# The w_down product of a decoder layer's MLP: 19 of its 44 steps over pairs of k tiles by Strassen's seven block products

## The chip, the cores and the metric

One Trainium2 chip, of which the kernel uses one core. The metric is the device time of one execution in microseconds (us), as the median of several runs. Engines are named as in the profile: PE (TensorE, the matmuls), PEld (its weight loads), DVE (VectorE), ACT (ScalarE), POOL (GpSimd), SP (SyncE, which here issues the loads).

## What is computed

One hybrid decoder layer on a sequence of 256 tokens and 2048 channels, in float32: two attention branches, then a gated MLP with a causal convolution. The change concerns only the last line of it, the product with w_down:

```python
D_MODEL = 2048; SEQ = 256; D_FF = 5632
...
        h = rms_norm(x, ffn_norm_g)
        u = causal_depthwise_conv(h @ w_up, conv_w, conv_b)
        gate, val = jnp.split(u, 2, axis=-1)
        x = x + (jax.nn.silu(gate) * val) @ w_down
    return x
```

## The kernel before

Every weight matrix streams through the same four-slot pipeline of chunks. A chunk is 128 partitions by 1024 float32 columns (512 KB). SP loads it into `raw[slot]`; ACT copies it to `hi[slot]` in the rounded matmul format (line 417); DVE subtracts, `lo = raw - hi` (line 740); PE then uses both. A float32 product is made of three matmuls with 512 moving columns: x_hi with w_hi, x_lo with w_hi, x_hi with w_lo, added up in one PSUM bank. All of PE's matmuls of the stage are recorded at line 1346 (`mm`). The semaphores that order this are counts over all chunks: `w_landed` (load finished), `hi_done`, `lo_done`, and `w_used` (PE has finished with the chunk). SP loads chunk c once `lo_done` shows that the chunk before it in the same slot has been split; ACT's split of chunk c waits until PE has used chunk c - 4. So the splits run at most three chunks ahead of PE.

The left operand of the w_down product is `ffT`: 44 tiles (k) of 128 channels by 256 tokens, its hi parts in columns 0 to 255 and its lo parts in columns 256 to 511. The product has two halves m of 1024 output columns. In each, PE goes over the 44 k tiles, one chunk of w_down each, and for each makes 4 products (2 token halves t by 2 column groups g), of 3 matmuls each, into the four banks `A[2 * t + g]`: 12 matmuls a chunk. At the end of a half DVE adds each bank to `y`, which holds the residual (`add_rows`, line 1103), and the first matmul of a bank in half 1 waits for that addition (`free_down`). SP stores `y` last. The banks `B` stand idle in this stage.

During the first eleven chunks of the stage the end of the up-projection still runs beside it (`up_step`): POOL multiplies the last four tiles (lines 1310, 1313, 1327, 1331), DVE does the convolution's taps (line 1051) and splits the last tiles of `ffT` (line 1058), ACT writes their hi parts (line 687).

```python
            for m in range(2):
                ...
                for k in range(FT):
                    if m == 0:
                        pe.wait_ge(ffT_done, k + 1)
                    rows_chunk(C_DOWN + FT * m + k + 1, k % SLOTS, ffT, [k], BLOCK,
                               [(A[2 * t + g], t, g * GRP, (g + 1) * GRP)
                                for t in range(TH) for g in range(2)], k == 0,
                               k == FT - 1, free_down, down_full)
```

Of the kernel before, what the change touches and what calls it, by code (L numbers as in the profile page):

```python
# [20 lines left out]

# [7 lines left out]
def hybrid_layer(nc, x, positions, attn_norm_g, w_in, q_norm_g, k_norm_g, w_branch, w_out,  # L29
# [9 lines left out]
    P = 128  # L39
# [35 lines left out]
    C_DOWN = C_UP + NU * 2 * CPG  # L75
    for first in (C_ROWS, C_HEADS, C_GATES, C_BRANCH, C_OUT, C_UP, C_DOWN):
        assert first % SLOTS == 0
# [9 lines left out]
    with ctx:  # L87
# [111 lines left out]
        silu = [at(f"silu{i}", [S], U0 + (13 + i) * KB) for i in range(4)]  # L199

# [130 lines left out]
        out_ready = sem("out_ready")  # L331
# [25 lines left out]
        def _(sp):  # L357
# [37 lines left out]
            with sp.Fori(0, 2) as m:  # L395
                load_group(C_DOWN, w_down, FT * m, BLOCK * m, n=FT, width=BLOCK, per=1)
            for m in range(2):
                for t in range(TH):
                    for h in range(2):
                        cols = slice(m * BLOCK + h * GRP, m * BLOCK + (h + 1) * GRP)  # L400

                        sp.wait_ge(out_ready, 4 * m + 2 * t + h + 1)
                        sp.dma_start(out[0, t * P:(t + 1) * P, cols], y[:, t, cols])\
                            .then_inc(stored, 16)
# [4 lines left out]
        def _(act):  # L409
# [312 lines left out]
            LAST = 3 * SLOTS  # L722
            for j in range(LAST):
                split(C_DOWN + AHEAD + j)
                up_step(NU, j)
            left = 2 * FT - AHEAD - LAST
            with act.Fori(0, left // SLOTS) as r:
                for j in range(SLOTS):
                    split(C_DOWN + AHEAD + LAST + j, r)
            for j in range(left - left % SLOTS, left):  # L730
                split(C_DOWN + AHEAD + LAST + j)


        @block.vector
        def _(dve):
# [357 lines left out]
            LAST = 3 * SLOTS  # L1093
            for j in range(LAST):
                split(C_DOWN + AHEAD + j)
                up_step(NU, j)

            def add_rows(m):
                for t in range(TH):
                    for g in range(2):  # L1100
                        cols = y[:, t, m * BLOCK + g * GRP:m * BLOCK + (g + 1) * GRP]
                        wait_full(dve, down_full, m, 4, 2 * t + g, C_DOWN + FT * (m + 1))
                        dve.tensor_tensor(cols, A[2 * t + g][:, :], cols, ALU.add)\  # L1103
                            .then_inc(out_ready, 1)

            first = C_DOWN + AHEAD + LAST
            with dve.Fori(0, (FT - LAST) // SLOTS) as r:
                for j in range(SLOTS):
                    split(first + j, r)
            add_rows(0)  # L1110
            second = first + FT - LAST
            left = FT - AHEAD
            with dve.Fori(0, left // SLOTS) as r:
                for j in range(SLOTS):
                    split(second + j, r)
            for j in range(left - left % SLOTS, left):
                split(second + j)
            add_rows(1)


        @block.gpsimd
        def _(pool):
# [217 lines left out]
            val_tiles(NU - 1)  # L1340


        @block.tensor
        def _(pe):
# [313 lines left out]
            for m in range(2):  # L1658
                def free_down(o):
                    if m == 0:  # L1660
                        pe.wait_ge(col_done, 64 + 4 * NU)
                    else:
                        pe.wait_ge(out_ready, 4 * (m - 1) + o + 1)
                for k in range(FT):
                    if m == 0:
                        pe.wait_ge(ffT_done, k + 1)
                    rows_chunk(C_DOWN + FT * m + k + 1, k % SLOTS, ffT, [k], BLOCK,
                               [(A[2 * t + g], t, g * GRP, (g + 1) * GRP)
                                for t in range(TH) for g in range(2)], k == 0,
                               k == FT - 1, free_down, down_full)  # L1670
# [22 lines left out]
```

## Time and profile before

| | |
|---|---|
| median of 3 runs | 1466.05 us (1465.93 to 1466.65) |
| the profiled execution's own time | 1466.32 us |
| its span, first to last instruction | 1464.3 us |
| PE busy | 1455.5 us, 99% of the span, 7688 matmuls |
| DVE busy | 932.5 us, 64% |
| ACT busy | 768.0 us, 52% |
| POOL busy | 431.1 us, 29% |
| mean DMA traffic | 186 GB/s |
| granted PE clock, mean | 0.999 |

Matmuls overlap in the pipeline, so one has a recorded duration of about 390 ns while they start much closer together; the pace has to be read from the starts. A busy share is an average over stages; what counts for this change is what the engines do in the last 240 us, where the w_down product runs. In the rows, "idle before" is the time an engine stood still before an instruction, with what released it.

### The profile page before, as it was taken

The numbers are of one execution on the slowest core, as the hardware profiler recorded it, in microseconds if no ns is written. First come the engines' busy times: TensorE is split into PE (matmuls) and PEld (weight loads), VectorE is DVE, ScalarE is ACT, GpSimd is POOL, SyncE is SP. The second block draws the span as 40 slices with busy tenths as digits, with TensorE's granted clock in tenths as the row PEclk, the third lists the DMA queues.
The fourth block names the chain that finished last, engine by engine and source line by source line (L and its number), as shares of the span: only waits on it lengthen the run. The fifth ranks groups of instructions, "written<-read, shape, count | busy, mean of one in ns | idle before, by whom it ended". The sixth has DMA issues, their size and how long they took to land.

```text
span 1464.3 us, 24546 instructions
## 1 busy us (share of the span) xinstructions
PE 1455.5 (99%) x7688; PEld 1246.4 (85%) x7688; DVE 932.5 (64%) x1205; ACT 768.0 (52%) x1063; POOL 431.1 (29%) x486
## 2 busy tenths in 40 slices
PE   8999999999999999999999999999999999999999
PEld 6888888888888888888888888888888888888887
DVE  6545455876655557765567778777777777545443
ACT  6544445576766766655454554454554555333332
POOL 1100000323222223550015555655555655000000
PEclk9999999999999999999999999999999999999999
DMA  7666665655555555575566666666666666655554
GB/s 243 194 181 186 186 180 165 193 179 177 158 167 158 158 169 176 186 246 186 186 186 177 198 188 186 185 187 194 193 188 192 179 191 198 201 194 191 190 197 147
DMA packets 130489, 272.09 MB, mean 186 GB/s; under 512 B 10784, under 2 KB 10816, under 8 KB 130192
## 3 DMA queue, kind: packets, MB, share of 16 engines
q1 hardware_dynamic: 129664, 269.12, 59.8%
q0 software_dynamic: 464, 2.42, 0.5%
q8 instruction: 25, 0.41, 0.1%
q14 instruction: 16, 0.13, 0.0%
q10 hardware_dynamic: 320, 0.01, 0.0%
HBM read 269.42 MB, written 2.10 MB: 185 GB/s over the span
## 4 chain that ended last, share of the span: by engine, by line
PE 99%; DVE 0%; DMA 0%; ACT 0%; issue 0%; POOL 0%; DVEq 0%; ACTq 0%; POOLq 0%
PE bank L1346 98%; PE bank L1395 0%; DMA rows_in<-in_attn_norm_g 0%; PE bank L1529 0%; DVE y L1103 0%; PE bank L1569 0%; DVE hT L765 0%; PE bank L1489 0%; ACT hi L417 0%; ACT hT L434 0%; POOL rows_in L1123 0%; DVE lo L740 0%; PE bank L1446 0%; PE bank L1419 0%; PE bank L1476 0%
## 5 line engine op out<-in xcount | busy, mean ns | idle before, releaser
L740 DVE TENSOR_TENSOR lo<-raw,hi 128x1024 fp32r<-128x1024 f32 (+1 forms) x508 | 651.0, 1285 | 425.0 <-ACT hi L417 424.2
L417 ACT ACTIVATE hi<-raw 128x1024 fp32r<-128x1024 f32 (+1 forms) x508 | 535.3, 1055 | 540.9 <-PE bank L1346 536.5
L1346 PE MATMUL bank<-h2T,hi 128*128 128x512 f32 x1408 | 482.8, 394 | 0.0
L1346 PE MATMUL bank<-h2T,lo 128*128 128x256 f32 x1408 | 376.4, 277 | 0.0
L1346 PEld LDWEIGHTS bank<-h2T,hi 128*128 128x128 f32 x1408 | 257.9, 188 | 53.4
L1346 PE MATMUL bank<-hT,hi 128*128 128x512 f32 (+1 forms) x784 | 274.4, 395 | 0.7 <-DVE lo L740 0.7
L1346 PEld LDWEIGHTS bank<-h2T,lo 128*128 128x128 f32 x1408 | 264.4, 188 | 7.8
L1346 PE MATMUL bank<-hi,ffT 128*128 128x512 f32 x704 | 216.8, 389 | 0.4 <-DVE y L1103 0.4
L1346 PE MATMUL bank<-hT,lo 128*128 128x256 f32 (+1 forms) x784 | 215.1, 284 | 0.0
L1346 PE MATMUL bank<-hi,hT 128*128 128x512 f32 x640 | 198.0, 390 | 0.0
L1310 POOL TENSOR_TENSOR u<-u,rms_row 128x256 f32<-128x256 f32 x88 | 121.3, 1378 | 237.9 <-DVE u L1041 220.6
L1346 PEld LDWEIGHTS bank<-hT,hi 128*128 128x128 f32 (+1 forms) x784 | 144.2, 187 | 30.3 <-DVE hT L765 1.0
L1346 PEld LDWEIGHTS bank<-hi,ffT 128*128 128x128 f32 x704 | 132.1, 188 | 28.1 <-DVE lo L740 0.8
L1346 PEld LDWEIGHTS bank<-hT,lo 128*128 128x128 f32 (+1 forms) x784 | 147.6, 188 | 4.2
L1051 DVE SCALAR_TENSOR_TENSOR conv<-u,params,conv 128x256 f32<-128x256 f32 x176 | 95.8, 544 | 76.8 <-POOL conv L1313 64.9
L1346 PEld LDWEIGHTS bank<-hi,hT 128*128 128x128 f32 x640 | 119.5, 188 | 24.6
L1346 PE MATMUL bank<-lo,ffT 128*128 128x512 f32 x352 | 136.9, 389 | 0.0
L1346 PE MATMUL bank<-lo,hT 128*128 128x512 f32 x320 | 124.6, 389 | 0.0
L1346 PE MATMUL bank<-oT,hi 128*128 128x512 f32 x256 | 88.2, 398 | 0.0
L1327 POOL TENSOR_TENSOR conv<-conv,params 128x256 f32<-128x256 f32 x44 | 63.5, 1444 | 61.7 <-DVE conv L1051 61.7
L1346 PE MATMUL bank<-hi,mT 128*128 128x512 f32 x256 | 80.0, 394 | 0.0
L1346 PEld LDWEIGHTS bank<-lo,ffT 128*128 128x128 f32 x352 | 66.1, 188 | 13.8
(198 smaller groups left out, 1224.9 us busy)
## 6 DMA issues: line engine op xcount, KB each, us to landing
raw<-in_w_in SPq DMA_DIRECT2D x176, 512.0 KB, 3.6
raw<-in_w_up SPq DMA_DIRECT2D x176, 512.0 KB, 3.8
raw<-in_w_down SPq DMA_DIRECT2D x88, 512.0 KB, 3.4
raw<-in_w_branch SPq DMA_DIRECT2D x32, 512.0 KB, 3.7
raw<-in_w_out SPq DMA_DIRECT2D x32, 512.0 KB, 3.6
y<-in_x SPq DMA_DIRECT2D x4, 512.0 KB, 7.0
y<-in_x POOLq DMA_DIRECT2D x1, 2048.0 KB, 9.5
out<-y SPq DMA_DIRECT2D x8, 256.0 KB, 3.1
```

The lines of the kernel that those rows point to most:

```text
L417: act.activation(hi[s][:, 0:width], raw[s][:, 0:width], ACT.Copy)\
L740: dve.tensor_tensor(lo[s][:, 0:width], raw[s][:, 0:width], hi[s][:, 0:width].bitcast(f32), ALU.subtract)\
L1051: dve.scalar_tensor_tensor(conv[b][ct % 2][:, :], u[b][ct][:, k:k + S], params[:, ds(column + e, 1)], conv[b][ct % 2][:, :], ALU.mult, ALU ...
L1310: pool.tensor_tensor(u[b][ct][:, 2:S + 2], u[b][ct][:, 2:S + 2], rms_row[:, :], ALU.mult).then_inc((gate_scaled, val_scaled)[b], 1)
L1327: pool.tensor_tensor(c, c, column(CONV_B + FT, e), ALU.add)\
L1346: return pe.matmul(o, l, r, start=start, stop=stop, skip_group_check=True)
```

## The change

The k tiles are taken in pairs, 22 in each half m, 44 steps. A plain step is as before: two chunks, 24 matmuls. In a summed step the pair of k tiles, the two token halves and the two column groups are treated as 2 x 2 blocks, and seven products of sums of blocks, by Strassen's scheme in its variant with shared sums, take the place of eight: 21 matmuls. Summed steps alternate with plain ones: 8 in half 0, after 6 plain steps, and 11 in half 1. `down_steps` writes the table `STEPS` from which all engines unroll their programs.

- A summed step has 4 chunks in the pipeline instead of 2: the first column group of the first weight tile (512 columns), the second tile (1024), and two sums of weight blocks, `sum13` and `sum24` (1024 each). DVE makes the sums from the raw tiles, four additions of 512 columns, during the plain step before (`sums13`, `sums24`); ACT and DVE split them like loaded chunks. SP reloads a raw slot only when the sums have been made from it.
- The left operand's sums are made once for each of the 11 pairs in `SUMMED` and used in both halves: POOL adds hi and lo (`whole`, 512 columns) and makes four differences or sums of 128 columns (`left_sums`), ACT rounds them (`left_hi_part`), DVE subtracts (`left_lo_part`, 128 and 384 columns). The first is wanted before step 6, then one every second step until step 25. The two buffers `left_raw` alternate.
- Four of the seven products go to the banks B, one to each, and the others to A[0], A[1] and A[2]. At the end of a half the B banks are combined and added to `y` (`add_p1`, `add_v5`, `make_u2_u3`, `add_u2_u3`): 12 DVE operations of 512 columns a half with `add_direct`, where there were 4, and one ACT copy. For half 0 they stand among DVE's splits of the first summed step of half 1; for half 1 at the very end, with the B banks first.

```diff
+    PAIRS = FT // 2
+    EARLY = 6
+    SUMMED = [*range(EARLY, EARLY + 8), 0, 1, 2]
...
+            def left_hi_part(i):
+
+                k = SUMMED[i]
+                act.wait_ge(left_full, i + 1)
+                if k < EARLY:
+                    act.wait_ge(w_used, STEPS[k].chunk + 2)
+                act.activation(ffT[:, 2 * k, P:S], left_raw[i % 2][:, 0, :], ACT.Copy)\
+                    .then_inc(left_hi, 1)
+                act.activation(left[k][:, :, 0, :], left_raw[i % 2][:, 1:4, :], ACT.Copy)\
+                    .then_inc(left_hi, 1)
...
+            def sums13(step):
+
+                for r in (step.raw, step.raw + 1):
+                    dve.wait_ge(w_landed[r % SLOTS], 16 * (r // SLOTS + 1))
+                if S_COUNT[step]:
+                    dve.wait_ge(lo_done, S_LIST[S_COUNT[step] - 1].chunk + 3)
+                b1, b2 = weights(step.raw), weights(step.raw + 1)
+                dve.tensor_tensor(sum13[:, 0:GRP], b1[:, 0:GRP], b1[:, GRP:2 * GRP], ALU.add)
+                dve.tensor_tensor(sum13[:, GRP:2 * GRP], b1[:, GRP:2 * GRP], b2[:, GRP:2 * GRP],
+                                  ALU.add).then_inc(sum13_done, 1)
...
+            def down_summed(step, combine):
+                down_lo(step.chunk, weights(step.raw), GRP)
+                if combine:
+                    add_v5(0)
+                down_lo(step.chunk + 1, weights(step.raw + 1))
+                if combine:
+                    make_u2_u3(0)
+                down_lo(step.chunk + 2, sum13)
+                if combine:
+                    add_direct(0)
+                down_lo(step.chunk + 3, sum24)
+                if combine:
+                    add_u2_u3(0)
...
+            def left_sums(i):
+
+                k = SUMMED[i]
+                f, d = whole[k], left_raw[i % 2]
...
+                if i >= 2:
+                    pool.wait_ge(left_done, 2 * (i - 1))
+                pool.tensor_tensor(f[:, :, :], ffT[:, 2 * k:2 * k + 2, 0:S].bitcast(f32),
+                                   ffT[:, 2 * k:2 * k + 2, S:2 * S].bitcast(f32), ALU.add)\
+                    .then_inc(whole_done, 1)
+                pool.wait_ge(whole_done, i + 1)
+                pool.tensor_tensor(d[:, 0, :], f[:, 0, P:S], f[:, 1, P:S], ALU.subtract)\
+                    .then_inc(left1_raw, 1)
+                pool.tensor_tensor(d[:, 2, :], f[:, 0, 0:P], f[:, 0, P:S], ALU.subtract)
+                pool.wait_ge(left1_raw, i + 1)
+                pool.tensor_tensor(d[:, 1, :], d[:, 0, :], f[:, 0, 0:P], ALU.subtract)\
+                    .then_inc(left2_raw, 1)
+                pool.wait_ge(left2_raw, i + 1)
+                pool.tensor_tensor(d[:, 3, :], d[:, 1, :], f[:, 1, 0:P], ALU.add)\
+                    .then_inc(left_full, 1)
...
+            def down_summed(step):
+                m, c, k, end = step.m, step.chunk, step.pair, step is S_LAST[step.m]
+                s2, s3, s4 = [(left[k][:, j, 0, :], left[k][:, j, 1, :]) for j in range(3)]
+                pe.wait_ge(lo_done, c + 1)
+                down_product(m, B[0], c, 0, *ff_part(2 * k, 0), end).then_inc(w_used, 1)
+                pe.wait_ge(lo_done, c + 2)
+                down_product(m, A[0], c + 1, 0, *ff_part(2 * k + 1, 0))
+                pe.wait_ge(left_done, 2 * step.made + 2)
+                down_product(m, A[1], c + 1, 1, *s4).then_inc(w_used, 1)
+                pe.wait_ge(lo_done, c + 3)
+                down_product(m, B[1], c + 2, 0, *ff_part(2 * k, 1), end)
+                down_product(m, B[3], c + 2, 1, *s3, end).then_inc(w_used, 1)
+                pe.wait_ge(lo_done, c + 4)
+                down_product(m, B[2], c + 3, 0, *s2, end)
+                down_product(m, A[2], c + 3, 1, *ff_part(2 * k + 1, 1)).then_inc(w_used, 1)
```

Three places show what the tables put on the engines. First, PE in the first summed step: `bank0` to `bank3` are A, `bank4` to `bank7` are B, and `left6` holds the left sums of pair 6.

```order
L1587 MATMUL bank4<-hi0_63,ffT_55 128x512 x2
L1587 MATMUL bank4<-lo0_67,ffT_55 128x512
L1587 MATMUL bank0<-hi1_64,ffT_55 128x512 x2
L1587 MATMUL bank0<-lo1_68,ffT_55 128x512
L1587 MATMUL bank1<-hi1_64,left6_176 128x512 x2
L1587 MATMUL bank1<-lo1_68,left6_176 128x512
L1587 MATMUL bank5<-hi2_65,ffT_55 128x512 x2
L1587 MATMUL bank5<-lo2_69,ffT_55 128x512
L1587 MATMUL bank7<-hi2_65,left6_176 128x512 x2
L1587 MATMUL bank7<-lo2_69,left6_176 128x512
L1587 MATMUL bank6<-hi3_66,left6_176 128x512 x2
L1587 MATMUL bank6<-lo3_70,left6_176 128x512
```

After these 18 matmuls one more product, into bank 2, ends the step; before, the same pair of k tiles had 24 matmuls in banks 0 to 3.

Second, DVE in half 0, from the plain step's first split to the end of the summed step's. Before, the same stretch was four splits of 128x1024 and nothing else.

```order
L1210 TENSOR_TENSOR lo0_67<-raw2_61,hi0_63 128x1024
L1225 TENSOR_TENSOR sum13_174<-raw0_59 128x512
L1226 TENSOR_TENSOR sum13_174<-raw0_59,raw1_60 128x512
L1210 TENSOR_TENSOR lo1_68<-raw3_62,hi1_64 128x1024
L1235 TENSOR_TENSOR sum24_175<-sum13_174,raw1_60 128x512
L1238 TENSOR_TENSOR sum24_175<-sum24_175,raw1_60 128x512
L1245 TENSOR_TENSOR ffT_55<-left_raw1_199,ffT_55 128x128
L1248 TENSOR_TENSOR left7_177<-left_raw1_199,left7_177 128x3x128
L1210 TENSOR_TENSOR lo2_69<-raw0_59,hi2_65 128x512
L1210 TENSOR_TENSOR lo3_70<-raw1_60,hi3_66 128x1024
L1210 TENSOR_TENSOR lo0_67<-sum13_174,hi0_63 128x1024
L1210 TENSOR_TENSOR lo1_68<-sum24_175,hi1_64 128x1024
```

Four sums, two left splits and one and a half more weight splits have come in between.

Third, DVE at the change of halves, in the first summed step of half 1. Before, four additions (banks 0 to 3) stood between two splits.

```order
L1258 TENSOR_TENSOR y_54<-y_54,bank4 128x512
L1210 TENSOR_TENSOR lo0_67<-raw0_59,hi0_63 128x512
L1258 TENSOR_TENSOR y_54<-y_54,bank5 128x512 x2
L1210 TENSOR_TENSOR lo1_68<-raw1_60,hi1_64 128x1024
L1272 TENSOR_TENSOR u2_sum_200<-bank6,u2_sum_200 128x512
L1275 TENSOR_TENSOR u3_sum_201<-bank7,u2_sum_200 128x512
L1210 TENSOR_TENSOR lo2_69<-sum13_174,hi2_65 128x1024
L1258 TENSOR_TENSOR y_54<-y_54,bank0 128x512
L1258 TENSOR_TENSOR y_54<-y_54,bank1 128x512
L1258 TENSOR_TENSOR y_54<-y_54,bank2 128x512
L1258 TENSOR_TENSOR y_54<-y_54,bank3 128x512
L1210 TENSOR_TENSOR lo3_70<-sum24_175,hi3_66 128x1024
```

The additions of banks 0 to 3 now stand behind five others and three splits, and three more follow the last split shown.

## Rows read from the trace of the kernel before

**Rows 1.** The page: busy us and share of the span, with instructions, of each engine
```profile
PE 1455.5 (99%) x7688; PEld 1246.4 (85%) x7688; DVE 932.5 (64%) x1205; ACT 768.0 (52%) x1063; POOL 431.1 (29%) x486
```

**Rows 2.** Waits from 1200 to 1460 us: total us, times, longest
```profile
ACT hi L417 <- PE bank L1346: 138.1, 87, 2.3
DVE lo L740 <- ACT hi L417: 111.3, 77, 1.6
...
PE bank L1346 <- DVE y L1103: 0.4, 1, 0.4
```

**Rows 3.** Timeline, PE, change of halves: start us, us, then the instruction
```profile
1340.25 0.39 PE L1346 MATMUL bank<-lo,ffT 128*128 128x512 f32 x1
...
1341.02 0.70 PE L1346 MATMUL bank<-hi,ffT 128*128 128x512 f32 x2 [0.39 <-DVE y L1103]
```

**Rows 4.** Timeline, PE, inside the w_down product
```profile
1252.08 0.62 PE L1346 MATMUL bank<-hi,ffT 128*128 128x512 f32 x2
1252.53 0.39 PE L1346 MATMUL bank<-lo,ffT 128*128 128x512 f32 x1
1252.76 0.62 PE L1346 MATMUL bank<-hi,ffT 128*128 128x512 f32 x2
```

**Rows 5.** Busy by stretch: length, PE, PEld, DVE, ACT, POOL, clock, DMA share, GB/s
```profile
1250.00:1300.00 50.00, 50.00 (x222) 41.39 (x222) 23.21 (x20) 19.22 (x19) 0.00 (x0) 1.00 0.60 200
```

**Rows 6.** Timeline, ACT, one split of a chunk
```profile
1346.78 1.06 ACT L417 ACTIVATE hi<-raw 128x1024 fp32r<-128x1024 f32 x1 [1.66 <-PE bank L1346]
```

**Rows 7.** Timeline, DVE, around the change of halves
```profile
1333.61 1.23 DVE L740 TENSOR_TENSOR lo<-raw,hi 128x1024 fp32r<-128x1024 f32 x1 [1.49 <-ACT hi L417]
...
1340.19 2.48 DVE L1103 TENSOR_TENSOR y<-bank,y 128x512 f32<-128x512 f32 x4
1342.59 1.21 DVE L740 TENSOR_TENSOR lo<-raw,hi 128x1024 fp32r<-128x1024 f32 x1
```

**Rows 8.** Timeline, DVE, beside POOL's last tiles
```profile
1233.97 1.22 DVE L740 TENSOR_TENSOR lo<-raw,hi 128x1024 fp32r<-128x1024 f32 x1
1235.11 0.83 DVE L1058 TENSOR_TENSOR ffT<-conv,ffT 128x256 fp32r<-128x256 f32 x1
1235.87 1.76 DVE L740 TENSOR_TENSOR lo<-raw,hi 128x1024 fp32r<-128x1024 f32 x1
...
1240.91 0.84 DVE L1058 TENSOR_TENSOR ffT<-conv,ffT 128x256 fp32r<-128x256 f32 x1
```

**Rows 9.** Timeline, POOL, the same stretch, and its last instruction
```profile
1235.74 0.80 POOL L1331 TENSOR_TENSOR conv<-conv,silu 128x256 f32<-128x256 f32 x1
1236.51 1.62 POOL L1310 TENSOR_TENSOR u<-u,rms_row 128x256 f32<-128x256 f32 x1
...
1247.34 0.80 POOL L1331 TENSOR_TENSOR conv<-conv,silu 128x256 f32<-128x256 f32 x1
```

**Rows 10.** Groups of POOL by shape: busy us, mean ns, then idle before
```profile
L1166 POOL TENSOR_TENSOR qn<-rot_d 128x256 f32<-128x256 f32 x4 | 3.0, 741 | 0.3
...
L1166 POOL TENSOR_TENSOR iq<-rot_i 128x128 f32<-128x128 f32 x4 | 1.8, 461 | 0.3
...
L1166 POOL TENSOR_TENSOR k_ix<-rot_k 128x64 f32<-128x64 f32 x1 | 0.3, 322 | 0.1
```

**Rows 11.** The end: last matmul in the timeline; last piece of the chain
```profile
1460.60 0.39 PE L1346 MATMUL bank<-lo,ffT 128*128 128x512 f32 x1
...
1458.98 2.73 DVE y L1103 x4
```

**Rows 12.** DMA, 1253 to 1337 us: queue's packets, MB, share; issues, KB, us to landing
```profile
q1 hardware_dynamic: 4475, 16.30, 57.8%
...
raw<-in_w_down SPq DMA_DIRECT2D x31, 512.0 KB, 3.4
```

**Rows 13.** Busy by stretch at the kernel's start, columns as in rows 5
```profile
0.00:5.00 5.00, 2.20 (x11) 2.20 (x12) 0.00 (x0) 1.49 (x2) 4.14 (x15) 1.00 0.58 175
5.00:10.00 5.00, 3.40 (x20) 2.33 (x19) 1.64 (x5) 2.41 (x8) 3.09 (x23) 0.96 0.93 266
10.00:15.00 5.00, 5.00 (x25) 3.66 (x24) 3.17 (x9) 4.00 (x11) 0.00 (x0) 0.70 1.04 315
```

More of the change, by code:

```diff
@@ L20 @@
 import math
+from collections import namedtuple
 import numpy as np
@@ L394, in _ @@
                     load_group(C_UP + b * CPG, w_up, 2 * CPG * n, b * FF + GRP * n)
-            with sp.Fori(0, 2) as m:
-                load_group(C_DOWN, w_down, FT * m, BLOCK * m, n=FT, width=BLOCK, per=1)
+            for i, step in enumerate(STEPS):
+                for k in range(2):
+                    if i < 2:
+                        wait_alone(sp, lo_done, step.raw + k - AHEAD)
+                    else:
+                        old = STEPS[i - 2]
+                        wait_alone(sp, lo_done, old.chunk + k + 1)
+                        if old.made is not None:
+                            wait_alone(sp, (sum13_done, sum4_done)[k], S_COUNT[old] + 1)
+                    kt = 2 * step.pair + k
+                    load((step.raw + k) % SLOTS, raw[(step.raw + k) % SLOTS][:, :],
+                         w_down[kt * P:(kt + 1) * P, step.m * BLOCK:(step.m + 1) * BLOCK])
             for m in range(2):
@@ L721, in _, with down_hi @@
                 up_body(n, True)
[L722 to L731, printed above, removed]
+            def down_hi(c, src, width=2 * GRP):
+                act.wait_ge(w_used, c - SLOTS + 1)
+                act.activation(hi[c % SLOTS][:, 0:width], src[:, 0:width], ACT.Copy)\
+                    .then_inc(hi_done, 1)
+                up_step(NU, c - C_DOWN - AHEAD)
@@ L1106, in _ @@
[L1106 to L1117, printed above, removed]
@@ new lines, in down_plain @@
+            def down_plain(step, after):
+                for k in range(2):
+                    if step.chunk + k >= C_DOWN + AHEAD:
+                        down_lo(step.chunk + k, weights(step.raw + k))
+                    if after is not None:
+                        (sums13, sums24)[k](after)
+            def down_summed(step, combine):
[11 more added lines that the diff above has]
+                    add_u2_u3(0)
@@ new lines, in _ @@
+            for i, step in enumerate(STEPS):
+                if step.made is None:
+                    after = STEPS[i + 1] if i + 1 < len(STEPS) else None
+                    down_plain(step, after if after is not None and after.made is not None
+                               else None)
+                else:
+                    down_summed(step, i == PAIRS)
+                if i >= EARLY - 1 and i % 2 == 1 and (i - EARLY + 1) // 2 < len(SUMMED):
+                    left_lo_part((i - EARLY + 1) // 2)
+                if i in (PAIRS - 1, 2 * PAIRS - 1):
+                    add_p1(step.m)
@@ L1121, in _ @@
+            add_v5(1)
+            make_u2_u3(1)
+            add_u2_u3(1)
+            add_direct(1)
         @block.gpsimd
@@ L1673 @@
+            for i, step in enumerate(STEPS):
+                if step.made is None:
+                    down_plain(step, i in (PAIRS - 1, 2 * PAIRS - 1))
+                else:
+                    down_summed(step)
 _INS = ["x", "positions", "attn_norm_g", "w_in", "q_norm_g", "k_norm_g", "w_branch", "w_out",
```

204 lines of the change are left out of this document (180 added, 24 removed).

## The prediction

> **What bounds the kernel now.** The page's busy shares come first [rows 1]: TensorE 99%, VectorE 64%. The chain of waits names TensorE for nearly everything, so the next question is whether TensorE ever waits in the w_down product. The waits of 1200 to 1460 us say it hardly does [rows 2]: ScalarE waited 138.1 us for TensorE to give a slot back and VectorE 111.3 us for ScalarE, while the matmul side lost one pause at the middle, where bank 0 had to be added to y first [rows 3]: 1340.25 + 0.39 to 1341.02, and in pace 0.54 us. So the stage is as long as its matmuls. Three of them start every 0.68 us [rows 4], 0.2267 us each, 2.72 us a chunk of 12; 88 chunks and the pause make 239.9 us, which places the stage's first matmul near 1220.9 and its end near 1460.8. The granted clock is 1.00 there [rows 5], the 2.4 GHz level. Of such a chunk's 2.72 us ScalarE uses 1.06 [rows 6] and VectorE 1.14 to 1.23 [rows 7].
>
> **The gain.** A summed step has 7 products of 3 matmuls for 8, so it issues 21 for 24. 19 x 3 x 0.2267 = **12.9 us** less TensorE work, 0.68 us per summed step. If nothing else mattered the kernel would come out at 1453.4.
>
> **What VectorE gets instead.** VectorE's price has two parts. Four adds of 512 columns and the next split start within 2.40 us [rows 7], so an operation of 512 columns occupies 0.60. A 1024-column split holds it 1.14, from 1233.97 to the 1235.11 of the next row [rows 8]. From both: 1.055 ns a column and 0.06 fixed. The added operations with both inputs in SBUF are not in the trace in this size; the bounds are 0.57 (half a split) and 0.69 (the recorded duration of one add, nothing overlapped), and I take 0.60, the start-to-start of the nearest row. A pair of a summed and a plain step then costs VectorE: five full splits 5.70, one half split and four sums 3.00, the left split of 128 and 384 columns 0.66, and 0.12 for the last sum, which waits for the one before. That is 9.5 us, and TensorE's pair takes 45 x 0.2267 = 10.2. So far it fits.
>
> **The turn it shares with POOL.** In the up-projection VectorE's split of 1235.87 took 1.76 instead of 1.22, with POOL's 256-column product started at 1235.74; POOL's next one (1236.51, 1.62 us for work that takes about 0.74 undisturbed) ended 0.59 after that split gave way [rows 8, 9, 10]. Each waits for the other when both read two SBUF tensors. The delay of 0.54 is what a 256-column POOL operation holds: 2.18 ns a column, the slope of POOL's 64-, 128- and 256-column rows [rows 10], with nothing fixed. The Trainium skill's page "SBUF — State Buffer" (SBUF: two separate sides) says the same more sharply, an exclusive lock for the whole instruction; by that the hold would be 0.74 and this sum 1489 (an estimate), but the measured 0.54 decides here.
>
> The change gives POOL 11 left parts, each one operation of 512 and four of 128 columns, 1024 columns: 1.10 + 4 x 0.26 = 2.1 us of hold. They depend on each other and are double buffered, so while VectorE is busy back to back each falls between two of its instructions and is paid in full. The pair is then 9.5 + 2.1 = **11.6 us of VectorE for 10.2 of TensorE**, and two plain steps cost 10.9 before. Only three chunks may be split ahead, so no reserve lasts.
>
> I walked all engines' orders with these prices, an instruction starting when its engine, its semaphores and the shared turn are free. (Laid on the old order the same walk spaces the L1058 operations 5.89 us; the rows have 1235.11 and 1240.91, 5.80 [rows 8].) Its subtotals:
> - First half, 8 pairs at 11.63 for 10.88: **+6.0**.
> - Entry: ScalarE stands at the left part of pair 6 while POOL, busy until 1247.34 + 0.80 = 1248.14 [rows 9], makes it; five operations (1.3 + 4 x 0.46 = 3.1) and its waits for VectorE end it near 1253, when TensorE is through chunk 11 (1220.9 + 12 x 2.72 = 1253.5). TensorE waits 1.1 for the next chunk; with no lead left, the early hold of the second left part (2.1), the last L1058 (0.34) and ScalarE's wait bring **+4.2**.
> - Middle: the pair at the change of halves has 12 bank additions (before 4): 12 x 0.60 = 7.2. VectorE needs 9.5 + 2.1 + 7.2 = 18.8 for TensorE's 10.2, and 0.9 of it may trail. Queued behind them are the splits of the first new chunks, and A[0] of the new half waits for its add. **+7.7**, less the old pause of 0.5 (the walk's 0.44).
> - Second half: the left parts are all made by then, a pair costs VectorE 9.5 or less, TensorE runs free: 11 x 0.68 = **-7.5**.
> - End: before, bank 3's add ended at 1461.71, 0.8 to 0.9 after the last matmul's columns (1460.60 + 0.23) [rows 11]. Now, from its last split 5.3 us before the end, VectorE does 8 additions (5.1 with waits) and then the 4 of banks 0 to 3 (2.4 less the overlap): 1.9 after. **+1.1**.
> The first half's +10.2 already contains its 8 gains. Sum: 10.2 + 7.7 - 0.4 - 7.5 + 1.1 = **+11.1**. The profiled execution took 1466.32 (span 1464.3), so 1477.4; the median of the runs is 0.27 lower, and I say **1477.2**.
>
> Priced at nothing: ScalarE, 6144 columns a pair at 1.06 per 1024 make 6.4 of 10.2 us; if that cover went, the hi of a chunk would be late next. Loads: a load lands 3.4 us after issue, and at 57.8% share 16.30 MB in 84 us make 1.6 us of transfer [rows 12]. The two raws of a summed step are issued right behind the splits of two steps earlier, 1.1 apart, and the sums want them 4 to 5 us later, so they just arrive. SyncE's queue has as many loads as before, but each summed step's reuse waits for the sums; if landings took 4.4 us (two transfers in a row), the total would be 1481.9.
>
> **The rivals.**
> 1. *POOL's work costs VectorE nothing* (it fits in VectorE's pauses, or sums in this form don't collide). Then 9.5 < 10.2, only middle, end and the bursts of full splits cost: the same walk without holds gives -6.7, **1459.6, faster**. For it: VectorE is idle a third of the stage now. Against: VectorE's pauses vanish just where POOL works. It decides at 0.7 us a pair: with a hold per left part under 0.7 instead of 2.1 TensorE is the bound. 11%.
> 2. *Shorter holds*, 0.41 for 256 columns, as the delay of L1058 in the rows (0.83 for about 0.42) may be read: **1471.5**. *Longer or slower*: holds of 0.64, 1484.7; adds at 0.63, 1482; late loads, 1481.9. 8% beyond 1485, the whole-instruction hold (1489) among it.
> 3. *The clock falls.* After ten microseconds with TensorE 2.2 and 3.4 of 5 us busy, the granted clock was 0.70 in the next five [rows 13], so partly at 1.2 GHz. Each 5 us at that level would do half the work: 2.5 us. Here TensorE stays 85% busy with pauses of 1 to 3 us, so I expect 1.00; a few falls would give 1480 to 1485. 5%. The Trainium skill's page "TensorE: Matmul & The Clock Gate" (Part 1) has the clock halve after an idle window.
> 4. *The change doesn't do what it says.* The order has 7 products in a summed step, so the 57 matmuls do go; at a pace other than 0.2267 1 ns is 1 us. Under 2%.
>
> **How the numbers follow.** Forecast, slower by 11 with its bounds (1470 to 1485): 0.76. Still slower beyond: 0.10. Rival 1, faster: 0.11. Between, within 0.2% or 2.9 us (about what a measurement of this kernel can tell from no change): 0.03. Range for 8 in 10: 1469 to 1485; own range of the likeliest 1471.5 to 1482. Faster 0.11, same 0.03, slower 0.86.
>
> **What would show it.** Right: POOL rows of 1.3 and 0.5 us stretched by VectorE between 1248 and some 1350; VectorE busy nearly without pause there; TensorE waiting for lo about 1.4 us a pair, one wait of about 3 us for y at the middle, none in the second half; bank additions ending 1.9 after the last matmul. Wrong: TensorE at 99% before the middle, or its waits going to loads or to ScalarE rather than VectorE.

## The result and the profile after

| | before | after |
|---|---|---|
| median of the runs | 1465.99 us (1465.91 to 1466.65) | **1484.45 us** (1483.59 to 1485.77) |
| the profiled execution's own time | 1466.32 us | 1483.59 us |
| its span | 1464.3 us | 1481.9 us |
| granted PE clock, mean | 0.999 | 0.996 |

The ratio is **1.0126, 95% interval 1.0108 to 1.0143**: 18.5 us slower by the medians, 17.3 by the profiled executions. The forecast was 1477.2 in a range of 1469 to 1485: the side was right and the size 7.3 us short.

The page's busy shares of the changed kernel, to set beside [rows 1]:

```profile
PE 1453.4 (98%) x7631; PEld 1235.6 (83%) x7631; DVE 1045.7 (71%) x1357; ACT 804.9 (54%) x1125; POOL 501.8 (34%) x541
```

57 matmuls are gone and 152 VectorE operations have come; averaged over the whole span, 71% would not look like a bottleneck. The last part of the span shows it. The waits from 1200 to 1482 us (total us, times, longest), beside [rows 2]:

```profile
ACT hi L795 <- PE bank L1587: 93.0, 63, 6.4
...
PEld bank L1587 <- DVE lo L1210: 31.8, 44, 4.9
DVE sum L1225 <- issue: 15.2, 11, 2.5
PE bank L1587 <- DVE lo L1210: 14.3, 14, 1.6
ACT ffT L810 <- POOL left_raw L1577: 12.5, 2, 9.1
...
PE bank L1587 <- DVE y L1258: 4.5, 1, 4.5
```

Before, VectorE waited 111.3 us for ScalarE, and a matmul waited once, for 0.4 us (a weight load once, for 0.8). Now TensorE waits for VectorE's lo, its weight loads (PEld) above all, and once for y. ScalarE's wait for POOL at the entry was in the forecast too. One wait was priced at nothing there: VectorE ahead of its sums, 15.2 us, "issue" being a wait of which the profile shows no releaser. The chain of waits, an excerpt (start, us, what), says what the latter is:

```profile
1391.15 5.04 DMA raw<-in_w_down
1396.18 1.32 issue
1397.50 0.13 DVE sum L1225
```

A sum needs two loaded tiles. The load of the first is in the chain. The second is issued 1.14 us behind it, at 1392.29, and lands 5.1 us later, at 1397.4, just before the sum starts; VectorE was ready for it at 1395.69, 3.4 us after the issue. So the second load's slack is as long as the old median landing, and it now takes longer. The nine landings in the chain from 1371 to 1465 take 3.24 to 5.04 us, five of them over 4.3, where [rows 12] have a median of 3.4.

**First half.** VectorE's timeline over one pair of steps, and POOL's beside it:

```profile
1305.28 2.92 DVE L1210 TENSOR_TENSOR lo<-raw,hi 128x512 fp32r<-128x512 f32 x2
1308.12 2.88 DVE L1210 TENSOR_TENSOR lo<-sum,hi 128x1024 fp32r<-128x1024 f32 x2
1310.92 1.48 DVE L1210 TENSOR_TENSOR lo<-raw,hi 128x1024 fp32r<-128x1024 f32 x1
...
1316.92 2.92 DVE L1210 TENSOR_TENSOR lo<-raw,hi 128x512 fp32r<-128x512 f32 x2
```

```profile
1305.44 1.67 POOL L1566 TENSOR_TENSOR whole<-ffT 128x512 f32<-128x512 f32 x1 [4.37 <-DVE left L1248]
1307.19 1.32 POOL L1570 TENSOR_TENSOR left_raw<-whole 128x128 f32<-128x128 f32 x1
1308.48 1.44 POOL L1572 TENSOR_TENSOR left_raw<-whole 128x128 f32<-128x128 f32 x1
1309.88 1.44 POOL L1574 TENSOR_TENSOR left_raw<-left_raw,whole 128x128 f32<-128x128 f32 x1
1311.40 1.32 POOL L1577 TENSOR_TENSOR left_raw<-left_raw,whole 128x128 f32<-128x128 f32 x1
```

A row with x2 joins two splits and names the shape of the first: the row of 2.92 is one of 512 and one of 1024 columns. It comes at 1281.98, 1293.63, 1305.28, 1316.92, 1328.57 and 1340.20: a pair takes **11.65 us**, and VectorE hardly pauses in it. Each POOL operation of 128 columns is recorded at 1.3 to 1.4 us, three times its undisturbed 0.46 [rows 10], which fits a wait for the running VectorE operation to end; the splits beside them are longer too (1.48 for 1.22, 2.92 where the second half has 1.82).

**Change of halves.** TensorE's timeline, beside [rows 3], and the stretches' busy times (columns as in rows 5):

```profile
1352.83 0.39 PE L1587 MATMUL bank<-lo,ffT 128*128 128x512 f32 x1
1354.13 0.73 PE L1587 MATMUL bank<-hi,ffT 128*128 128x512 f32 x2 [0.91 <-DVE lo L1210]
...
1359.61 1.19 PE L1587 MATMUL bank<-hi,ffT 128*128 128x512 f32 x2 [4.51 <-DVE y L1258]
```

```profile
1358.00:1360.00 2.00, 0.39 (x1) 0.42 (x2) 2.00 (x4) 0.00 (x0) 0.00 (x0) 0.50 0.59 213
1360.00:1362.00 2.00, 2.00 (x6) 1.52 (x6) 2.00 (x4) 0.00 (x0) 0.00 (x0) 0.50 0.00 0
```

One pause of 4.5 us where there was one of 0.4, and a granted clock of 0.50, the 1.2 GHz level, from inside the pause to 1362 (0.67 in the two us after that). VectorE is busy all through: it has the 12 additions and four splits to do. Its own pair at this place, from the first split of half 1 to that of the next summed step, takes 16.91 us:

```profile
1352.68 1.39 DVE L1210 TENSOR_TENSOR lo<-raw,hi 128x512 fp32r<-128x512 f32 x1
...
1369.59 1.82 DVE L1210 TENSOR_TENSOR lo<-raw,hi 128x512 fp32r<-128x512 f32 x2
```

**Second half and end.** Nine pairs, from the split at 1369.59 to the one at 1465.15, take 95.6 us: 10.62 each, where TensorE needs 10.2. In the middle of one of them VectorE stands still for a load:

```profile
1394.48 1.22 DVE L1210 TENSOR_TENSOR lo<-raw,hi 128x1024 fp32r<-128x1024 f32 x1
1397.50 0.69 DVE L1225 TENSOR_TENSOR sum<-raw 128x512 f32<-128x512 f32 x1 [1.81 <-issue]
```

The last matmul and the last additions, beside [rows 11]:

```profile
1476.79 0.39 PE L1587 MATMUL bank<-lo,ffT 128*128 128x512 f32 x1
```

```profile
1476.58 2.47 DVE L1258 TENSOR_TENSOR y<-y,bank 128x512 f32<-128x512 f32 x4
```

**Where the 17.3 us came from**, each stretch read from one record to the same one in the other trace: the last matmul of half 0 ends at 1353.22 where it ended at 1340.64, **+12.6**; from there to the last matmul's end, 1477.18, takes 123.96 where it took 120.35, **+3.6**; from there to the last addition, 1.87 against 0.72, **+1.1**.

### The profile page after: what moved, and what is told of

The parts are those of the page before. It is cut to its first block and busy times, and to the rows that moved or that the text cites. A ratio compares the mean times of both kernels' runs of the same rounds, so it can differ in the third digit from the quotient of the medians.

```text
span 1481.9 us, 24362 instructions
## 1 busy us (share of the span) xinstructions
PE 1453.4 (98%) x7631; PEld 1235.6 (83%) x7631; DVE 1045.7 (71%) x1357; ACT 804.9 (54%) x1125; POOL 501.8 (34%) x541
## 5 line engine op out<-in xcount | busy, mean ns | idle before, releaser
L853 DVE TENSOR_TENSOR lo<-raw,hi 128x1024 fp32r<-128x1024 f32 (+1 forms) x423 | 544.9, 1292 | 314.5 <-ACT hi L486 313.7
L486 ACT ACTIVATE hi<-raw 128x1024 fp32r<-128x1024 f32 (+1 forms) x423 | 445.0, 1054 | 408.4 <-PE bank L1587 403.5
L1587 PE MATMUL bank<-hi,ffT 128*128 128x512 f32 x552 | 174.6, 398 | 19.0 <-DVE lo L1210 14.3
L1587 PEld LDWEIGHTS bank<-hi,ffT 128*128 128x128 f32 x552 | 101.5, 189 | 49.8 <-DVE lo L1210 30.6
L1587 PE MATMUL bank<-lo,ffT 128*128 128x512 f32 x276 | 108.4, 393 | 0.0
L1210 DVE TENSOR_TENSOR lo<-raw,hi 128x1024 fp32r<-128x1024 f32 x85 | 104.9, 1251 | 2.7 <-ACT hi L795 2.6
L795 ACT ACTIVATE hi<-raw 128x1024 fp32r<-128x1024 f32 x85 | 81.5, 960 | 44.2 <-PE bank L1587 32.7
```

Of the source, the lines that this page charges most:

```text
L486: act.activation(hi[s][:, 0:width], raw[s][:, 0:width], ACT.Copy)\
L795: act.activation(hi[c % SLOTS][:, 0:width], src[:, 0:width], ACT.Copy)\
L853: dve.tensor_tensor(lo[s][:, 0:width], raw[s][:, 0:width], hi[s][:, 0:width].bitcast(f32), ALU.subtract)\
L1210: dve.tensor_tensor(lo[s][:, 0:width], src[:, 0:width], hi[s][:, 0:width].bitcast(f32), ALU.subtract)\
L1587: return pe.matmul(o, l, r, start=start, stop=stop, skip_group_check=True)
```

## The experiments

The theory was the prediction's: VectorE bounds the first half, because it pays the turns of POOL on top of its own work; the middle is the sum of VectorE's additions. Added after the result: what the forecast missed is loads that come late for the sums. The rivals are named at each run. All times are medians; the kernel before had 1466.5 to 1466.6 beside them. The changed kernel was not run again beside them: its 1484.45 belongs to 1465.99 for the kernel before, so a time "less" or "more" than it is uncertain by some 0.5 us from that alone. Diffs are against the changed kernel unless something else is said, and are excerpts.

### 1. POOL makes two of the eleven left parts

```diff
-                act.wait_ge(left_full, i + 1)
+                act.wait_ge(left_full, min(i + 1, 2))
...
-            for i in range(len(SUMMED)):
+            for i in range(2):
```

> The changed kernel with POOL making only the first two left parts; ScalarE and VectorE round the same two buffers again for the other nine, so TensorE's sums of ffT are not the right ones, while every other instruction, wait and load stays. Theory (each POOL operation takes its turn out of VectorE's time): nine parts of 2.1 us of hold leave the first half, a pair there falls from 11.65 us to 10.2 to 10.4, which is TensorE's 45 matmuls or VectorE's own 9.5 plus the wait for late loads; about 8 to 12 us less than the changed kernel's 1484.5, so 1473 to 1477. Rival (POOL works in VectorE's pauses, the first half is slow for another reason, such as loads): within 1 us of 1484.5.

Measured: **1475.97** (1475.82 to 1478.06), ratio 1.0069 (1.0052 to 1.0085); 8.5 us less. VectorE's timeline of a pair, with what ended its pauses:

```profile
1290.73 1.82 DVE L1210 TENSOR_TENSOR lo<-raw,hi 128x512 fp32r<-128x512 f32 x2
...
1293.96 1.23 DVE L1210 TENSOR_TENSOR lo<-sum,hi 128x1024 fp32r<-128x1024 f32 x1 [0.27 <-ACT hi L795]
...
1296.69 0.69 DVE L1225 TENSOR_TENSOR sum<-raw 128x512 f32<-128x512 f32 x1 [0.37 <-issue]
...
1301.04 1.82 DVE L1210 TENSOR_TENSOR lo<-raw,hi 128x512 fp32r<-128x512 f32 x2
```

The two splits of the x2 row, of 512 and 1024 columns, are back from 2.92 to 1.82 and VectorE pauses again. This pair takes 10.31; between 1280 and 1340 TensorE is busy 59.84 of 60 us, where the changed kernel has 54.66. The average from 1279.78 to 1333.94 is 10.83 a pair, more than the 10.2 to 10.4 expected: in three of these five pairs VectorE waits 1.3 us ahead of a sum. The pauses ahead of the sums (22.4 us in the whole stage) show the loads as next in line.

### 2. The same sums made by VectorE itself

The five operations of `left_sums` are moved word for word from POOL's program to VectorE's, one step ahead of the left split that uses them.

```diff
+                if i >= EARLY - 2 and i % 2 == 0 and (i - EARLY + 2) // 2 < len(SUMMED):
+                    left_sums((i - EARLY + 2) // 2)
...
-            for i in range(len(SUMMED)):
-                left_sums(i)
```

> The left parts' five operations moved from POOL to VectorE, one step ahead of their rounding. VectorE gets 11 x (1.07 + 5 x 0.06 + waits, together about 1.6 us) of its own, 18 us more instructions on the engine that is the bound of the first half. Theory (a part on POOL costs VectorE 2.1 us of turn, more than the same work done by itself): a pair of the first half goes from 11.65 to about 11.1, and ScalarE no longer waits for POOL at the start (4 us); 1475 to 1480. Rival (POOL's work costs VectorE little): the pairs grow to 12 or more, 1490 to 1497.

Measured: **1478.91** (1477.56 to 1479.07), ratio 1.0082 (1.0065 to 1.0099). VectorE's timeline:

```profile
1303.93 0.68 DVE L1262 TENSOR_TENSOR whole<-ffT 128x512 f32<-128x512 f32 x1
...
1305.38 0.29 DVE L1273 TENSOR_TENSOR left_raw<-left_raw,whole 128x128 f32<-128x128 f32 x1
1305.59 1.22 DVE L1210 TENSOR_TENSOR lo<-raw,hi 128x1024 fp32r<-128x1024 f32 x1
```

All five take 1305.59 - 1303.93 = 1.66 us of VectorE, and leaving them to POOL costs VectorE 2.16 (11.65 less the 9.5 that experiment 7 measures): moved off the busy engine, this work was dearer for that engine than doing it. This pair, 1299.92 to 1311.06, takes 11.14, the 0.5 less that the two prices ask for; two of the five pairs up to 1333.94 have a late load in them and take 11.6 and 11.7. More of the gain lies at the entry, where the wait for POOL is gone: the first of these rows comes at 1277.14, 4.8 us earlier than in the changed kernel. Half 0 ends 6.6 us earlier, and 1.6 of them are lost again in half 1.

### 3. Short loads for the summed steps

The loads of summed steps bring 256 of 1024 columns; nothing else changes, and the products of those steps are made from partly stale tiles.

```diff
+                    width = BLOCK if step.made is None else BLOCK // 4
```

> The two loads of each summed step bring 256 of 1024 columns (128 KB for 512 KB); the other columns keep what an earlier load left, so the summed steps compute with wrong weights. Theory: the sums in VectorE's program wait for raws that land 4.4 to 5 us after issue because up to three 512 KB transfers are in flight; with short ones the waits before the sums (15.2 us in all, 0.4 to 2.5 each) mostly go, and the second half, where TensorE is the bound, comes down by 3 to 5 us: 1479 to 1481, with the first half's pair at 11.65 unchanged. Rival (the second half is late from the clock and VectorE's backlog at the middle, its load waits lie in VectorE's slack): 1483 to 1485.

Measured: **1478.08** (1478.0 to 1479.02), ratio 1.0081 (1.0064 to 1.0098): 6.4 us less. The first half's pair stays at 11.65 (1280.74, 1292.39, 1304.04), the waits ahead of the sums are gone, the second half's pair takes 10.20, and TensorE is busy 60.00 of 60 us between 1400 and 1460, where it was 58.88. These loads land 2.4 us after issue, the full ones between them 3.6 (medians, 1370 to 1440).

### 4. TensorE kept busy at the change of halves

Sixteen matmuls whose result is overwritten are issued into the free bank B[0] while TensorE would stand still.

```diff
                     if o == 4:
                         pe.wait_ge(p1_copied, 1)
+                        for _ in range(16):
+                            mm(bank[:, :], xh, hi[c % SLOTS][:, 0:GRP], True, True)
```

> Sixteen extra matmuls of 512 columns in bank B[0] just before its first product of the second half resets it; nothing computed changes. They last 3.6 us of the 4.5 us that TensorE waits at the middle. Theory: TensorE's pause of 4.5 us there lets the granted clock fall to 0.50 from about 1357 to 1363, and the matmuls issued at that level cost twice: without the fall 1.5 to 2 us less, 1482.5 to 1483, and granted clock 1.00 in that stretch. Rival (VectorE's queue alone sets when the second half gets going, the slow matmuls hide behind it): no change within 0.5 us, 1484 to 1485, or up to 1 us more if the extra matmuls delay the first chunk's release.

Measured: **1484.83** (1481.51 to 1485.89), ratio 1.012 (1.0104 to 1.0137): no change that four executions with 4.4 us between them can tell. The granted clock did stay up (busy times of the stretch, of this kernel and then of the changed one):

```profile
1353.00:1365.00 12.00, 9.84 (x40) 7.34 (x41) 11.97 (x17) 4.66 (x7) 2.48 (x4) 1.00 0.25 88
```

```profile
1353.00:1365.00 12.00, 6.58 (x20) 4.85 (x20) 11.96 (x16) 4.36 (x6) 3.56 (x5) 0.72 0.27 88
```

With the clock at 1.00 the pause only moves: TensorE waits 1.29 us for lo at 1364.22, where the changed kernel had no wait. VectorE is busy 11.97 and 11.96 of these 12 us, and its pair at the middle takes 16.92 us (1351.50 to 1368.42) for 16.91: the slow matmuls had been hidden behind it.

### 5. The direct banks first

Two of the four direct additions are put ahead of four of the B banks' additions and of one split (the expectation says five; the first addition, of B[0], stays ahead), and two behind them.

```diff
                 down_lo(step.chunk + 1, weights(step.raw + 1))
                 if combine:
-                    make_u2_u3(0)
+                    add_direct(0, [0])
+                    add_v5(0)
```

> In VectorE's program at the change of halves the additions of banks 0 and 1 move ahead of five others and of one split, so A[0] is free about 3 us earlier. The same 12 additions and the same splits. Theory (it is the sum of VectorE's work there that delays TensorE, 7.2 us of additions on an engine with no slack, not their order): the pause of 4.5 us shortens and comes back as waits for lo; 1483.5 to 1485.5. Rival (the order costs, and with the pause the fall of the clock): 1480 to 1482.

Measured: **1485.86** (1484.18 to 1486.5), ratio 1.0133 (1.0117 to 1.0148): no gain. TensorE's pauses of the middle in its timeline:

```profile
1356.19 0.70 PE L1589 MATMUL bank<-hi,ffT 128*128 128x512 f32 x2 [1.13 <-DVE y L1258]
...
1359.22 0.73 PE L1589 MATMUL bank<-hi,ffT 128*128 128x512 f32 x2 [1.39 <-DVE lo L1210]
...
1365.82 0.73 PE L1589 MATMUL bank<-hi,ffT 128*128 128x512 f32 x2 [2.47 <-DVE lo L1210]
```

One pause of 4.51 (and 0.91 ahead of it) became six of 0.80, 1.13, 1.39, 0.37, 0.17 and 2.47: 6.3 in all for 5.4, now at a granted clock of 1.00 throughout (1352 to 1370). VectorE's pair there takes 17.37 us (1352.65 to 1370.02), 0.5 more than before the reordering. What the stretch costs is how much VectorE has to do, not which bank comes first.

### 6 and 7. Summed steps in the second half alone, with four and with six raw slots

In experiment 6 half 0 is all plain steps, and the 11 summed steps are those of half 1; the left parts are made along the way. Experiment 7 gives the loads two more slots from the 33rd on, in memory that is free by then.

```diff
-    SUMMED = [*range(EARLY, EARLY + 8), 0, 1, 2]
+    SUMMED = [*range(PAIRS // 2)]
...
-        first = [(0, k, None) for k in range(EARLY)]
+        first = [(0, k, None) for k in range(PAIRS)]
```

```diff
+    USES, FIVE = [[] for _ in range(6)], 32
+    for n in range(2 * FT):
+        USES[n % 4 if n < FIVE else (n - FIVE) % 6].append(n)
```

> Half 0 all plain, 11 summed steps in half 1 only: 33 matmuls fewer than before instead of 57. POOL makes its 11 parts in half 0, where VectorE idles over a third, and the middle has 4 additions as in the kernel before. Theory: no bound by VectorE in half 0 (its steps at 5.44 us each, the holds hidden), no queue in the middle; -7.5 for the matmuls, +1.2 at the end, and about 0.4 us a pair of late loads in half 1 (4 to 5 us, as the runs with all 19 show there): 1463.5 to 1466 against 1466.3 for the kernel before. Rival (summed steps cost VectorE more than TensorE gains wherever they stand): slower than before, 1468 to 1475.

> The same with six raw slots instead of four from the 33rd load of the stage on (two buffers of 4 KB where the up-projection's tiles were, the end's two sums in the place of the weight sums), so a load is issued one step earlier. Theory: the waits for late raws go, half 1's pairs take 10.2 us: -7.5 + 1.2 and 0.5 for what is left, 1459.5 to 1461. Rival (the waits before the sums are not for loads, or the DMA queue's rate bounds them): within 1 us of the run with four slots.

Measured: **1463.88** (1462.98 to 1466.21, 10 runs), ratio 0.9984 (0.9974 to 0.9993), and **1460.62** (1460.33 to 1460.82, 5 runs), ratio 0.996 (0.9946 to 0.9973). In experiment 6 the pairs of half 1 take 10.5 us, with nine waits ahead of the sums (12.0 us). In experiment 7 they take exactly 10.20, the starts being 1389.72, 1399.92, 1410.12; VectorE's timeline of one:

```profile
1399.92 1.82 DVE L1218 TENSOR_TENSOR lo<-raw,hi 128x512 fp32r<-128x512 f32 x2
1401.65 1.22 DVE L1218 TENSOR_TENSOR lo<-sum,hi 128x1024 fp32r<-128x1024 f32 x1
1404.17 1.23 DVE L1218 TENSOR_TENSOR lo<-sum,hi 128x1024 fp32r<-128x1024 f32 x1 [1.30 <-ACT hi L805]
...
1410.12 1.82 DVE L1218 TENSOR_TENSOR lo<-raw,hi 128x512 fp32r<-128x512 f32 x2
```

VectorE's only pause is for ScalarE, which waits for TensorE: TensorE is the bound, busy 50.00 of 50 us from 1400 to 1450. The row also measures VectorE's own price of such a pair: 10.20 less the pause of 1.38 (from 1401.65 + 1.14 to 1404.17) is 8.8, and with the left split's 0.67 it is **9.5**.

### 8. The changed kernel with a fifth slot

One slot more from the 17th load on (the same table as in experiment 7, `(n - 16) % 5`).

> The changed kernel, 19 summed steps and right weights, with a fifth raw slot from the 17th load of the stage on. Theory: the same gain as with short loads, since both only bring the raws in time: 1477 to 1480, first half's pair at 11.65, second half's at 10.2. Rival (short loads helped by moving fewer bytes, for instance through the transfers' own rate): 1482 to 1485.

Measured: **1478.6** (1477.83 to 1479.15), ratio 1.008 (1.0065 to 1.0095): 5.9 us less with every transfer in full. The first half's pair stays 11.65, the second half's becomes 10.20 (1388.12, 1398.32, 1408.52), and TensorE is busy without a gap (stretch of this kernel, then of the changed one):

```profile
1400.00:1450.00 50.00, 50.00 (x223) 41.39 (x222) 43.34 (x51) 28.34 (x30) 0.00 (x0) 1.00 0.63 205
```

```profile
1400.00:1450.00 50.00, 48.88 (x212) 39.39 (x212) 42.31 (x47) 27.77 (x29) 0.00 (x0) 1.00 0.63 200
```

The fifth slot doesn't make a landing shorter (median 4.2 us between 1370 and 1440, 4.0 without it); it lets the load be issued earlier.

### 9. Five additions at the change of halves

```diff
-    ORDER = [["11p1", "12v5", "22v5", "u2", "u3", "11p2", "12v3", "21q4", "22e8", "12u2", "21u3",
-              "22u3"],
+    ORDER = [["11p1", "11p2", "12v3", "21q4", "22e8"],
```

> The changed kernel with 5 bank additions at the change of halves where it has 12: the 7 operations that form u2 and u3 and add v5, u2 and u3 to y for the first 1024 output columns are left out (so these columns lack those products); every matmul, split and load stays. Theory (the pause at the middle is the sum of VectorE's additions, 0.60 us each): 7 x 0.60 = 4.2 us less, part of it perhaps eaten by the load waits behind it: 1480 to 1482, and TensorE's wait for y of 4.51 us shrinks to under 1. Rival (the pause is the price of the order, of one late addition or of the change of slots): 1484 or more, the wait for y as long as before.

Measured: **1480.68** (1479.8 to 1481.17), ratio 1.0095 (1.0078 to 1.0112): 3.8 us less for seven operations, 0.54 each. TensorE's timeline:

```profile
1353.45 0.73 PE L1579 MATMUL bank<-hi,ffT 128*128 128x512 f32 x2 [0.77 <-DVE lo L1208]
...
1356.93 0.70 PE L1579 MATMUL bank<-hi,ffT 128*128 128x512 f32 x2 [2.52 <-DVE y L1256]
```

The wait for y went from 4.51 to 2.52, not under 1 as expected: of the seven operations only four stood ahead of the direct additions, 4 x 0.60 = 2.4 us, and the wait shrank by 2.0. The other three stood behind, where they held up the next splits. The expectation had counted all seven into the pause. VectorE's pair at the middle takes 13.13 us (1351.98 to 1365.11) for 16.91, again 0.54 for each of the seven; in this trace the nine pairs behind it then take 10.85 instead of 10.62, with late loads, and give 2.1 of the 3.8 us back.

### 10. The matmuls alone

The kernel before, with 57 matmuls fewer and nothing in their place.

```diff
+                    if k % 4 == 1 and k // 4 < (8, 11)[m]:
+                        outs = outs[:3]
```

> The kernel before, with the last of four products (3 of 12 matmuls) left out in 19 of its 88 chunks, 8 in the first half and 11 in the second; nothing is added in their place, so part of the product is missing from the output. It measures the gain term alone. Theory: 57 x 0.2267 = 12.9 us less, 1453.2 to 1454.0. Rival (TensorE's matmuls are not the whole of the bound: the slots, the splits or the loads take some back): 1456 or more.

Measured: **1453.68** (1453.6 to 1453.81), ratio 0.9913 (0.9897 to 0.993): 12.8 us less, 0.2243 a matmul. The gain term stands, and nothing else of the stage would have held it back.

### 11. POOL's largest operation done twice

```diff
                 pool.wait_ge(whole_done, i + 1)
+                pool.tensor_tensor(f[:, :, :], ffT[:, 2 * k:2 * k + 2, 0:S].bitcast(f32),
+                                   ffT[:, 2 * k:2 * k + 2, S:2 * S].bitcast(f32), ALU.add)\
+                    .then_inc(whole_twice, 1)
```

> The changed kernel, with POOL's 512-column operation of each left part done twice with the same result. It doubles the suspected cost of the shared turn: by 2.18 ns a column a hold of 1.1 us more per left part. Theory (VectorE pays every hold in the first half): the first half's pair goes from 11.65 to about 12.7, and with 8 or 9 such parts the time to 1492 to 1495. Rival 1 (POOL's work falls into VectorE's pauses): 1484.5, pair 11.65. Rival 2 (the hold is the whole recorded duration, 1.3 to 1.5 us): 1496 or more.

Measured: **1493.35** (1492.59 to 1493.91), ratio 1.0182 (1.0165 to 1.0199): 8.9 us more. VectorE's timeline, a pair, and POOL's added operation:

```profile
1297.89 2.92 DVE L1211 TENSOR_TENSOR lo<-raw,hi 128x512 fp32r<-128x512 f32 x2
1300.73 3.71 DVE L1211 TENSOR_TENSOR lo<-sum,hi 128x1024 fp32r<-128x1024 f32 x2
...
1310.63 2.92 DVE L1211 TENSOR_TENSOR lo<-raw,hi 128x512 fp32r<-128x512 f32 x2
```

```profile
1299.80 2.16 POOL L1571 TENSOR_TENSOR whole<-ffT 128x512 f32<-128x512 f32 x1
```

The pair takes 12.74 for 11.65. One POOL operation of 512 columns, recorded at 2.16 us, takes **1.09 us** from VectorE: 2.13 ns a column, and 8 such pairs make the 8.7 of the 8.9 us. The two splits beside it went from 2.88 to 3.71. Rival 1 would have left the pair at 11.65, rival 2 asked for 1.3 or more.

## Why the prediction was right, and 7 us short

- **The gain, -12.9.** Right: 12.8 when nothing is put in its place (experiment 10).
- **VectorE's own pair, 9.5.** Right: 9.5 in experiment 7. The 0.60 of an addition with both inputs in SBUF is confirmed there (1406.45 to 1407.05 in that trace).
- **POOL's holds, 2.1 a pair.** Right: 11.65 less the 9.49 of experiment 7 is 2.16 in place, 1.09 for the 1.10 of the 512-column operation by itself (experiment 11), and with the holds gone the first half's pair falls to 10.31 at its best and 10.83 on average, the rest being late loads (experiment 1). (1024 columns at 2.18 ns would be 2.23; the working's 1.10 and 0.26 follow the delay of 0.54, 2.11 ns a column.) Rival 1, the faster case, fell with these three runs. The Trainium skill's page "SBUF — State Buffer" (SBUF: two separate sides) names an exclusive lock for the whole instruction; the exclusion is seen here, but what VectorE loses is 1.09 us where the extrapolation of [rows 10] to 512 columns (0.74 + 256 x 2.18 ns) has a whole instruction at 1.30, so the measured hold decides. Whether the lock is shorter than the instruction, or a part of the instruction runs beside VectorE's, no run tells.
- **First half, pair at 11.63.** It is 11.65. Half 0 as a whole was forecast at +10.2 and came out at +12.6: **2.4 too little**. With short loads that half ends 1.3 earlier (at 1351.9 instead of 1353.2): VectorE's wait of 1.26 ahead of the sum at 1277.64, a late load, is gone, and its next pair starts at 1280.74 instead of 1281.98. That wait is not the same in every execution: in the trace of experiment 4, with the same program up to there, it is 0.34, and half 0 ends at 1352.2. Where the other 1.1 lies no run takes apart; TensorE's first two pauses at the entry are 1.59 and 0.68 where one of 1.1 was forecast.
- **Middle, +7.7, less 0.4.** About right in size, wrong in form. The forecast for the stretch from the half's last matmul to the end was 7.7 - 0.4 - 7.5 = -0.2 and it came out at +3.6; without late loads it is -0.6 (experiment 3) and +0.6 (experiment 8), so the loads hold the difference (next point). The pause was 4.5, with one of 0.9 for lo ahead of it, and not "about 3". Experiment 9 prices the additions at 0.54 each where 0.60 was taken.
- **Second half, -7.5, "TensorE runs free".** This is the term that was too good, with the one behind it, **loads priced at nothing**: "they just arrive". They don't. Nine pairs took 10.62 instead of 10.2, 3.8 us in all. Both experiments that remove only the late loads (3 and 8) give pairs at TensorE's own pace and 6.4 and 5.9 us, most of the 7.3 that were missing; their 1478.1 and 1478.6 are where the forecast of 1477.2 had put the kernel. The prediction did have the case, landings of 4.4 us, at 1481.9, but took the median landing of the old kernel, 3.4 [rows 12], for loads that are now issued in close groups, and counted "4 to 5 us later" from the first of the two, where the second has 3.4 (1392.29 to 1395.69). The measured 1484.45 also lies where rival 3 put a few falls of the clock; experiments 4 and 5 rule out the fall at the middle as its cause, and 3 and 8 show the loads.
- **End, +1.1.** Right: 1.1 more between the records (1.9 after the last matmul's columns was forecast, 1476.58 + 2.47 less 1476.79 and 0.23 is 2.0).
- **The clock (rival 3).** It fell, against the forecast of 1.00, to 0.50 behind the pause of 4.5 us, and to 0.57 from 1257 to 1261, behind two of 1.59 and 0.68. The Trainium skill's page "TensorE: Matmul & The Clock Gate" (Part 1) has it halve after idle time, and for the pause of 4.5 us the trace agrees. But the price at the middle was nothing that shows: with the clock held at 1.00 (experiment 4) VectorE's pair there took the same time, and with the pause split up (experiment 5) nothing was gained, since TensorE was not the bound. For the fall at the entry no run holds the clock up with everything else kept.

So the forecast's structure held, and most of the missing 7 us, about 6 by the medians, has one cause: loads late for the sums. Of the rest, some 1.1 us of half 0 stay open. The experiments' parts overlap, and do not add up to the whole: without late loads the kernel is 6 us faster, without POOL 8.5, and each uncovers a part of the other.

## What to carry to other kernels

Price a change on every engine, above all when it takes work from the busy one: here a gain of 12.8 us that was real had to pay a VectorE whose share over the kernel was a harmless 64%. The scheme pays only where its additions fit under the matmuls. Of the versions run here that was the second half alone, by 0.16% with four load buffers and by 0.4% with two more (1460.62 us). And work that "just arrives" is a term with a size: a load whose slack is about its landing time has no reserve, and here one buffer more was worth 5.9 us.

## What the runs showed of the hardware beside that

- An engine can be relieved by giving it more work: the left sums take VectorE 1.66 us when it makes them itself and 2.16 when POOL does. Doubling POOL's largest operation cost VectorE 1.09 more (experiment 11), so it is POOL's operations with SBUF inputs that take turns with VectorE's.
- A POOL operation's recorded duration says little beside a busy VectorE: 128 columns are recorded at 1.32 to 1.44 us there and 0.46 alone, 512 columns at 1.67 or 2.16, for a hold of 1.09.
- The landing of a 512 KB load varies with what is issued around it. In the old stage one is issued every 2.72 us and the median is 3.4 us. In the second half of the changed kernel the median is 4.0; one issued alone at 1389.15 took 3.2, two issued at 1391.15 and 1392.29, while it was under way, 5.0 and 5.1. With short loads for the summed steps the full ones between them are at 3.6.
- The same pauses do not lower the clock at the same moment in every execution. At the entry the changed kernel and experiment 5 run the same program. TensorE pauses for 1.59 and 0.68 us before 1257, and for 1.44 and 1.26 before 1272; in experiment 5 for 1.60 and 0.67, and for 1.62 and 1.24. The changed kernel's clock fell behind the first two:

```profile
1257.00:1261.00 4.00, 3.85 (x10) 3.05 (x11) 4.00 (x5) 2.73 (x3) 3.42 (x2) 0.57 0.73 247
```

  and was 1.00 from 1269 to 1281. In experiment 5 it was 1.00 behind the first two and fell behind the next:

```profile
1257.00:1261.00 4.00, 3.43 (x14) 2.35 (x15) 4.00 (x4) 2.50 (x3) 3.67 (x3) 1.00 0.63 220
...
1273.00:1275.00 2.00, 2.00 (x7) 1.54 (x6) 2.00 (x3) 0.56 (x1) 2.00 (x2) 0.50 0.82 236
```

  Half 0 ended at 1353.2 and 1353.3. At the middle the clock was 0.50 behind the pause of 4.51, and in experiment 9 behind 0.77 and 2.52, but 1.00 through the six pauses of experiment 5.
